# Recurrence of a hybrid encoder: which operand of the level products is stationary, and the order of the jobs beside them

## What is computed

```
def step(S, inp):
    r_t, w_t, k_t, v_t, a_t, b_t = inp
    sa = jnp.einsum('bhvk,bhk->bhv', S, a_t)
    S_new = S * w_t[:, :, None, :] + sa[..., None] * b_t[:, :, None, :] + v_t[..., None] * k_t[:, :, None, :]
    y = jnp.einsum('bhvk,bhk->bhv', S_new if inclusive else S, r_t)
    return S_new, y
```

## Time and profile before

| | us |
|---|---|
| median of 3 runs | 1944.28 (1942.8 to 1944.61) |
| the profiled execution | 1947.11 |
| its span | 1945.0 |
| the recurrence in it, from the first A to the last Y | 316.0 |
| one of its later chunks | 37.6 |

### The profile page before, as it was taken

One profiled execution on the slowest core, in us unless ns is written; L12 is line 12 of the kernel. 1 busy time (PEld: TensorE's weight loads), 2 busy tenths in 40 slices (PEclk: granted clock), 3 DMA queues, 4 the chain that ended last, 5 costly groups with the idle time before them and its releaser, 6 DMA issues.

```text
span 1945.0 us, 22750 instructions
## 1 busy us (share of the span) xinstructions
PE 1763.7 (91%) x8988; PEld 1261.4 (65%) x8988; DVE 827.2 (43%) x1193; ACT 555.5 (29%) x1058; POOL 320.7 (16%) x263
## 2 busy tenths in 40 slices
PE   2999978789999996888888997999999999999995
PEld 2888736544444433676676444888888888888884
DVE  7224348765534426545553646211211121133555
ACT  3111167734343322433432012111111111122331
POOL 1700011146000004455452015200000000000000
PEclk8999999989999997788887998999999999999998
DMA  4310000000000000000001300411111111144333
GB/s 187 130 54 32 11 29 1 12 5 4 8 4 4 0 0 14 2 2 2 2 2 53 153 11 11 152 43 43 52 56 43 43 51 57 56 149 138 95 95 115
DMA packets 24277, 93.49 MB, mean 48 GB/s; under 512 B 2752, under 2 KB 5120, under 8 KB 23568
## 3 DMA queue, kind: packets, MB, share of 16 engines
q1 hardware_dynamic: 23744, 87.27, 13.0%
q0 software_dynamic: 464, 5.28, 0.7%
HBM read 79.92 MB, written 12.58 MB: 48 GB/s over the span
## 4 chain that ended last, share of the span: by engine, by line
PE 84%; DVE 9%; ACT 4%; issue 2%; DMA 1%; POOL 0%; SPq 0%; DVEq 0%; ACTq 0%; POOLq 0%
PE psum L1842 25%; PE psum L1868 12%; PE psum L1456 9%; PE psum L1597 5%; PE psum L1793 5%; PE psum L1607 5%; PE psum L1474 2%; PE psum L1556 2%; PE psum L1538 1%; PE psum L1579 1%; PE psum L1693 1%; PE psum L1519 1%; PE psum L1481 1%; DVE stats L1138 1%; PE psum L1761 1%
## 5 line engine op out<-in xcount | busy, mean ns | idle before, releaser
L1842 PE MATMUL psum<-h_hi,w_hi 128*128 128x512 f32 x704 | 275.2, 391 | 11.7 <-DVE h_lo L1336 11.7
L1842 PE MATMUL psum<-h_lo,w_hi 128*128 128x512 f32 x704 | 274.4, 390 | 0.0
L1842 PE MATMUL psum<-h_hi,w_lo 128*128 128x512 f32 x704 | 274.4, 390 | 0.0
L1369 DVE TENSOR_TENSOR arena<-psum,arena 128x1024 f32 (+1 forms) x22 | 27.0, 1225 | 391.3 <-ACT arena L914 391.3
L1842 PEld LDWEIGHTS psum<-h_hi,w_hi 128*128 128x128 f32 x704 | 132.6, 188 | 39.7 <-DVE h_lo L1336 12.0
L1842 PEld LDWEIGHTS psum<-h_lo,w_hi 128*128 128x128 f32 x704 | 132.6, 188 | 27.8 <-issue 0.2
L1842 PEld LDWEIGHTS psum<-h_hi,w_lo 128*128 128x128 f32 x704 | 132.5, 188 | 27.5
L628 POOL TENSOR_TENSOR arena<-arena,consts 128x512 f32<-128x512 f32 x64 | 80.2, 1270 | 321.9 <-ACT arena L846 321.9
L1868 PE MATMUL psum<-wd_hi,act_lo 128*128 128x512 f32 x336 | 130.7, 389 | 0.0
L1868 PE MATMUL psum<-wd_lo,act_hi 128*128 128x512 f32 x336 | 130.7, 389 | 0.0
L1868 PE MATMUL psum<-wd_hi,act_hi 128*128 128x512 f32 x336 | 130.7, 389 | 0.0
(11 more groups left out here) (265 smaller groups left out, 2895.8 us busy)
## 6 DMA issues: line engine op xcount, KB each, us to landing
arena<-in_w_down SPq DMA_DIRECT2D x44, 512.0 KB, 3.6
arena<-in_w_gate SPq DMA_DIRECT2D x22, 512.0 KB, 3.5
arena<-in_w_up SPq DMA_DIRECT2D x22, 512.0 KB, 4.6
arena<-in_w_in SPq DMA_DIRECT2D x15, 512.0 KB, 3.6
arena<-in_x SPq DMA_DIRECT2D x8, 512.0 KB, 10.1
resid_spill<-arena POOLq DMA_DIRECT2D x1, 4096.0 KB, 12.9
arena<-in_w_out SPq DMA_DIRECT2D x8, 512.0 KB, 6.2
arena<-resid_spill SPq DMA_DIRECT2D x1, 4096.0 KB, 19.5
```

Source lines behind the costliest of these rows:

```text
L1842: mm = pe.matmul(bank(4 * b + 2 * n + hf), w[b][n][:, P * k:P * k + P], x[k][:, cols], start=(k == 0 and i == 0), stop=(k == KT - 1 and i ...
```

## The change

A level has two hops left for each direction, G and E. In both the full 128x128 matrix of a head is stationary (Lev in G, Xt in E) and the compact 32 columns move (Xc in G, Gc in E). The result comes out in the layout in which it is wanted, so GT and D's second transpose are gone, with their ACT copies. Xc and Xtc exist twice, by the parity of the chunk, so that A of the next chunk can be taken up earlier. G5 takes Xc and D5 Xtc directly. The blocks of the full X and Xt are put in place by 12 small POOL copies for each chunk (own_blocks). G6 of both directions is one job, with the two directions' products in turn on different tiles of the array; so is D6. AV and AZ become one job AX that accumulates in PSUM, without a DVE addition. The jobs beside the chain get new places (BESIDE), U of the chunk before right behind G of level 1.

```diff
-HOPS = [(kind, m) for m in range(1, 5) for kind in ("G", "GT", "D", "E")] + [(kind, 0) for kind in ("G5", "D5", "G6", "D6")]
-BACK = {0: ("AZ0", "AZ1"), 1: ("U0",), 2: ("U1",), 3: ("Y0",), 4: ("Y1",), 5: ("S0",), 6: ("S1",)}
-FRONT = {7: ("tok0",), 8: ("V0", "V1"), 9: ("tok1",), 10: ("KR0",), 11: ("KR1",), 12: ("AV0",), 13: ("AV1",), 14: ("R0",),
-         15: ("R1",)}
-AHEAD = {16: ("A0",), 17: ("A1",)}
+HOPS = [(kind, m) for m in range(1, 5) for kind in ("G", "E")] + [(kind, 0) for kind in ("G5", "D5", "G6", "D6")]
+BESIDE = {0: ("U0-",), 1: ("U1-", "Y0-", "A0+"), 2: ("KR0",), 3: ("Y1-",), 4: ("KR1",), 5: ("A1+", "S0-", "S1-"),
+          6: ("V1",), 7: ("V0", "tok0"), 8: ("R0", "tok1"), 9: ("AX1",), 10: ("AX0",), 11: ("R1",)}
+TOGETHER = ("G6", "D6")
...
-            jobs += [(kind, d, m, i) for d in range(2)]
-            if i:
-                jobs += named(BACK.get(n, ()), i - 1)
-            jobs += named(FRONT.get(n, ()), i)
-            if i + 1 < NT:
-                jobs += named(AHEAD.get(n, ()), i + 1)
-    return jobs + named(("AZ0", "AZ1", "U0", "U1", "Y0", "Y1"), NT - 1)
+            if i < NT:
+                jobs += [(kind, d, m, i) for d in range(1 if kind in TOGETHER else 2)]
+            for name in BESIDE.get(n, ()):
+                j = i + name.count("+") - name.count("-")
+                kind_d = name.strip("+-")
+                if 0 <= j < NT and not (kind_d[0] == "S" and j == NT - 1):
+                    jobs.append((kind_d[:-1], int(kind_d[-1]), 0, j))
...
+        elif kind in TOGETHER:
+            banks[job] = (4 + turn[0], 6 + turn[1])
+            turn = [1 - turn[0], 1 - turn[1]]
...
-        Xc, Xtc, Gc, G5 = ([heads4(32) for d in range(2)] for _ in range(4))
-        Gr, Dr = ([small(P) for d in range(2)] for _ in range(2))
+        Xcs, Xtcs = ([[heads4(32) for d in range(2)] for n in range(2)] for _ in range(2))
+        Gc, G5 = ([heads4(32) for d in range(2)] for _ in range(2))
...
+            def own_blocks(full, compact, which, i):
+
+                for d in range(2):
+                    pool.wait_ge(xt_ready, XTC_AT[d, 4, i])
+                    rows64 = halves_of(d)[which]
+                    for at in (rows64.start, rows64.start + 32):
+                        rows = slice(at, at + 32)
+                        pool.tensor_copy(full[d][rows, :, rows], compact[d][rows]).then_inc(xt_full, 1)
...
+                if i:
+                    pool.wait_ge(xt_full, OTHER_HALF_AT[i - 1])
...
+                pool.wait_ge(xt_full, XT_AT[1, 4, i])
+                own_blocks(X, Xcs[i % 2], 1, i)
+                own_blocks(Xt, Xtcs[i % 2], 0, i)
+                own_blocks(X, Xcs[i % 2], 0, i)
...
-                elif kind in ("G", "GT", "D"):
-                    dst = {"G": Gr[d], "GT": Gc[d].rearrange("p h c -> p (h c)"), "D": Dr[d]}[kind]
-                    ins = act.activation(dst, psum[:, b0, 0:P], ACT.Copy)
-                elif kind == "E" and m == 4:
-                    taken(act, job)
-                    for p in range(4):
-                        rows = slice(32 * p, 32 * p + 32)
-                        act.activation(X[d][rows, :, 32 * p:32 * p + 32], Xc[d][rows], ACT.Copy).then_inc(x_full, 1)
+                elif kind == "G":
+                    ins = act.activation(Gc[d].rearrange("p h c -> p (h c)"), psum[:, b0, 0:P], ACT.Copy)
...
+                    if i >= 2:
+                        v.wait_ge(xt_full, OTHER_HALF_AT[i - 2])
...
-                    if m == 4:
-                        v.wait_ge(xt_ready, XTC_AT[d, m, i])
-                        v.tensor_tensor(Xt[d].rearrange("p h (k c) -> p h k c", c=32), spread(Xtc[d]), own_block,
-                                        ALU.mult).then_inc(xt_ready, 1)
...
-                elif kind == "AZ":
-                    taken(v, ("AV", d, 0, i))
-                    v.tensor_tensor(Xs[d].rearrange("p h c -> p (h c)"), bank(b0, 256),
-                                    AVs[d].rearrange("p h c -> p (h c)"), ALU.add).then_inc(out_v, 1)
...
-                        mm = pe.matmul(psum[32 * h:32 * h + 32, b0, 0:P], Xc[d][:, h, :], Lev[d][m % 2][:, h, :],
-                                       start=True, stop=True, skip_group_check=True)
-                elif kind in ("GT", "E"):
-                    taken(pe, ("G" if kind == "GT" else "D", d, m, i))
-                    mm = pe.transpose(quarter, (Gr if kind == "GT" else Dr)[d], ident)
-                elif kind == "D":
-                    taken(pe, ("GT", d, m, i))
+                        mm = pe.matmul(psum[:, b0, 32 * h:32 * h + 32], Lev[d][m % 2][:, h, :], Xc[d][:, h, :],
+                                       start=True, stop=True)
+                elif kind == "E":
+                    taken(pe, ("G", d, m, i))
                     pe.wait_ge(xt_full, XT_AT[d, m, i])
                     for h in range(4):
-                        mm = pe.matmul(psum[32 * h:32 * h + 32, b0, 0:P], Gc[d][:, h, :], Xt[d][:, h, :],
-                                       start=True, stop=True, skip_group_check=True)
+                        mm = pe.matmul(psum[:, b0, 32 * h:32 * h + 32], Xt[d][:, h, :], Gc[d][:, h, :],
+                                       start=True, stop=True)
...
+                elif kind in TOGETHER:
+                    if kind == "G6":
+                        taken(pe, ("D5", 0, 0, i))
+                        taken(pe, ("D5", 1, 0, i))
+                        pe.wait_ge(xt_full, FIRST_HALF_AT[i])
+                    else:
+                        taken(pe, ("G6", 0, 0, i))
+                        pe.wait_ge(xt_full, TURNED_OWN_AT[i])
+                        pe.wait_ge(xt_ready, TURNED_AT[1, i])
+                    for h in range(4):
+                        for d in range(2):
+                            dst, src = halves_of(d)
+                            out = psum[dst, banks[d], 64 * h:64 * h + 64]
+                            if kind == "G6":
...
-                elif kind == "AV":
+                elif kind == "AX":
                     taken(pe, ("KR", d, 0, i))
                     taken(pe, ("V", d, 0, i))
                     for h in range(4):
-                        mm = pe.matmul(psum[:, b0, 64 * h:64 * h + 64], KAm[d][:, h, :],
-                                       tokv[d][:, h // 2, 64 * (h % 2):64 * (h % 2) + 64], start=True, stop=True)
-                elif kind == "AZ":
+                        pe.matmul(psum[:, b0, 64 * h:64 * h + 64], KAm[d][:, h, :],
+                                  tokv[d][:, h // 2, 64 * (h % 2):64 * (h % 2) + 64], start=(h == 0), stop=False,
+                                  skip_group_check=True)
                     if i:
                         taken(pe, ("S", d, 0, i - 1))
                     else:
                         pe.wait_ge(y_cleared, 5)
                     for hp in range(2):
                         mm = pe.matmul(psum[:, b0, P * hp:P * hp + P], At[:, 2 * d + hp, at_chunk(d, i)], Zs[d][:, hp, :],
-                                       start=True, stop=True)
+                                       start=False, stop=True, skip_group_check=True)
```

More of the change, by code:

```diff
@@ L89 @@
 LEV_AT = {(d, m, i): 8 * i + 2 * (m - 1) + d + 1 for i in range(NT) for m in range(1, 5) for d in range(2)}
[L90 to L93, removed]
+XT_AT = {(d, m, i): 20 * i + 2 * (m - 1) + d + 1 for i in range(NT) for m in range(1, 5) for d in range(2)}
+XTC_AT = {(d, m, i): 10 * i + 2 * (m - 1) + d + 1 for i in range(NT) for m in range(1, 5) for d in range(2)}
+TURNED_AT = {(d, i): 10 * i + d + 9 for i in range(NT) for d in range(2)}
+FIRST_HALF_AT = {i: 20 * i + 12 for i in range(NT)}
+TURNED_OWN_AT = {i: 20 * i + 16 for i in range(NT)}
+OTHER_HALF_AT = {i: 20 * i + 20 for i in range(NT)}
 def bank_plan():
@@ L311, in hybrid_encoder @@
         at[1] += at[0]
-        AVs, Us = ([pairs2() for d in range(2)] for _ in range(2))
+        Us = [pairs2() for d in range(2)]
         G6 = [heads4(64) for d in range(2)]
@@ L862, in _ @@
                 elif kind == "G6":
-                    dst, src = halves_of(d)
-                    ins = act.activation(G6[d][dst].rearrange("p h c -> p (h c)"), psum[dst, b0, 0:256], ACT.Copy)
+                    for d in range(2):
+                        dst, src = halves_of(d)
+                        ins = act.activation(G6[d][dst].rearrange("p h c -> p (h c)"), psum[dst, BANKS[job][d], 0:256], ACT.Copy)
                 elif kind == "tok":
                     ins = act.activation(tokm[d].rearrange("p q s c -> p (q s c)"), bank(b0), ACT.Copy)
-                elif kind in ("V", "AV", "U"):
-                    dst = {"V": tokv, "AV": AVs, "U": Us}[kind][d]
+                elif kind in ("V", "AX", "U"):
+                    dst = {"V": tokv, "AX": Xs, "U": Us}[kind][d]
                     ins = act.activation(dst.rearrange("p h c -> p (h c)"), bank(b0, 256), ACT.Copy)
@@ L1260, in _ @@
                 elif kind == "D6":
-                    dst, src = halves_of(d)
```

(34 more changed lines are left out.)

28 lines of the change are left out of this document (13 added, 15 removed).

## The result

| | before | after |
|---|---|---|
| median of the runs, us | 1944.05 (1942.8 to 1944.61, 4 runs) | 2053.25 (2052.66 to 2072.74, 4 runs) |
| span of the profiled execution, us | 1945.0 | 2051.5 |
| the recurrence in it, us | 316.0 | 421.8 |

The change makes the kernel slower by 5.9%: the ratio is 1.0587, 95% interval 1.0525 to 1.0649. The span grew by 106.5 us and the recurrence alone by 105.8 us, so hardly anything else moved. One of the four executions took 2072.74 us, at a mean granted clock of 0.895 against 0.901 to 0.904 in the others.

The account below looks back on a forecast made before the run. PE's jobs, the waits between them and the half clock were taken to bound the kernel. The recurrence: 8.4 + 50.6 + 431.2 - 2.5 + 10.4 = 498.1 us against 316.0, 182 us more: 2126 us, range 1965 to 2150.

Parts of the forecast that it names:

- the load bounds the product: G and E: the 128-column weight load sets the time, so 32 moving columns don't shorten it; 114 ns an instruction.
- PE's work at both clocks: PE's jobs in a later chunk, summed: 33.9 us at full clock, 64.6 us at half.
- The waits: PE's waits within a chunk, 5.1 us before, were taken to vanish behind PE's own jobs.
- The sign that G6 of both directions would take less time than one had alone: G6 as one job on different tiles: both directions in less time than one alone before.
- Without the clock the change is worth 3.7 us a chunk: Later chunk of the recurrence: 37.6 us before less 33.9 us of PE work at full clock.
- The forecast's own case: Recurrence mostly at half clock, granted clock near 0.55, 498 us; kernel 2126 us; chance 0.58 together with half clock throughout.
- So a chunk takes 61.6 us: Later chunk: 64.6 us at half clock less 3 us for the clock returning around A, S0 and S1.
- E4: E of level 4, in the thin stretch where the returned clock was to be lost again; its return worth 3 us a chunk.
- rival 1: Clock returns at S, is lost at G of level 1: 50.9 us a chunk, 2053 us; chance 0.20.
- rival 2: Clock falls once a chunk for 10.2 us, as before: 39.0 us a chunk, 1967 us; chance 0.06.
- four half-clock cases: Recurrence mostly at half clock 2126 us, back from S to level 1 2053, one fall a chunk 1967, half throughout 2147.
- Rival 3: PE without waits gets full clock in the recurrence, keeping 3.7 us a chunk: 1917 us; chance 0.14.

Follow-up runs that it names:

- wide: Changed kernel with all 128 compact columns moving in G and E, only 32 of each head's result columns read: 1920.5 us.
- wide_g: Changed kernel with 128 columns moving in G only, E keeping 32: 1927.8 us.
- half: Changed kernel with 64 columns (two heads) moving in G and E, of which 32 are used: 1955.7 us.
- wide_serial: As wide, but G6 and D6 issued direction after direction inside their one job, not in turn: 1923.2 us.
- shift1: Changed kernel with one DVE memset added between the first A and the first level, to start the levels some 2 us later: 2061.9 us.
- shift2: Changed kernel with two DVE memsets added between the first A and the first level, to start the levels some 4 us later: 1988.2 us.

## Why the prediction was right, and where it wasn't

**The range and the direction** held: slower, 2053.25 us inside 1965 to 2150. The mechanism behind them, that the load bounds the product and that few streamed columns cost the clock, was right and is shown by wide, wide_g and half. What exactly the chip counts stays open: the columns that move past the array and the results that it writes grew together in these runs.

**PE's work at both clocks** was right. A level job was put at 0.91 and 1.70 us and took 0.86 and 1.71 (half of the 16 instructions of G, and 8 times 213 ns). A chunk at full clock was put at 33.9 us and took 34.8 in wide, 34.5 in half. At half clock it was put at 64.6; chunk 3 took 60.5 us with a clock of 0.53, which is 64 us for 0.50. Chunk 0 with what precedes it was put at 59.0 us and took 58.4.

**The waits** were taken at nothing, and PE had none from the first G to the last Y. POOL's 12 copies for a chunk took 289 ns each, against 286. Three terms of the sum at full clock were mis-sized, and cancel in the main: G6 and D6 took 0.61 us each against 0.45, the two AX 3.06 us against 2.7, G5 and D5 1.64 us against 2.2. The sign that G6 of both directions would take less time than one had alone didn't appear, as in wide_serial one direction alone takes half of 0.89 us.

**"Without the clock the change is worth 3.7 us a chunk"** sets a changed chunk at full clock, 33.9 us, against the 37.6 us of before, which hold 5.1 us of half clock's cost by the prediction's own count. Against 32.5 us, an estimate for a chunk of before at full clock throughout, the changed chunk is 1.4 us longer. By this estimate what wide gains on the kernel before comes from the clock as well.

**The forecast's own case was wrong.** The step that failed is "So a chunk takes 61.6 us", which a clock near 0.55 and 498 us for the recurrence follow from; measured were 0.63 and 421.8 us. I let the clock come back at S and be lost with G4, V1 and E4, worth 3 us. It did come back there, at 844.4 and 1015.1, but was then kept for 17 us, through E4, G5 and D5 to E of level 1. That is rival 1, chunks of 52.8 and 53.1 us against its 50.9. Others lost it at once: chunk 3 with 60.5 us is the forecast's case. And chunks 5 and 6 with 37.6 us, clock lost for 6.8 us only, are rival 2, which I had put at 39.0. So three of my four half-clock cases occurred side by side in one execution. The forecast, 182 us more, was 1.7 times the 109 measured.

**Rival 1's 2053 us is the measured time, by luck.** It assumed seven equal chunks of 50.9 us; the seven took 37.6 to 60.5, and only their mean is the same. shift1 and shift2 ran from 1984 to 2083 us with the same work. What I should have seen is that the case isn't fixed by the order of the jobs alone: the seven chunks have the same order. That the moment at which the clock changes against the jobs decides is my reading, and not shown by itself. A single number for this kernel was worth less than its range.

**Rival 3**, full clock throughout, was put at 1917 us for the changed kernel and didn't occur there. wide is that case made real, 1920.5 us. The rule of the Trainium skill that the prediction names beside it (TensorE: Matmul & The Clock Gate, The HAM clock gate), that a busy PE is released to full clock, doesn't hold in the row of 804.7 to 844.4: busy for 39.70 of 39.70 us, clock 0.50.

**What the prediction missed**: that the cure was in its own argument. If the load bounds the product, more moving columns, up to 128, are nearly free, and the clock they hold is worth 133 us.

## What to carry to other kernels

Where a weight load bounds a float32 product, moving more columns cost next to nothing here (107 ns an instruction with 32, 112 with 128; more than 128 wasn't tried there), and streaming too few cost the clock of the jobs around it as well; ask of a denser schedule how much it streams, not only whether the engine waits. A transposed product that saves hops can still lose if it gives up column strips that worked at once: here the old level products with the rest of the change are the fastest version. And when a chunk of equal work takes 37.6 us once and 60.5 us another time, repeat the run, and shift the work by a few microseconds, before believing a single measured number.

## What the runs showed of the hardware

- The clock can stay at 0.50 while PE is busy without a gap: 39.7 us in chunk 1 of the changed kernel. At the start of half it stayed there for 98.2 us with 91.87 us busy.
- The same stream of jobs can hold the full clock and fail to regain it: half, 98.2 us at 0.50, then 225.6 us at 1.00, with S of chunk 1 at the rise.
- A float32 instruction with 128 stationary columns takes 107 ns at full clock with 32 moving columns, 108 with 64 and 112 with 128. At half clock, 16 of them in a row took 3.55 us with 32 (with the first one's start), 3.60 with 64 and 3.71 with 128.
- The number of moving columns in the level products set the time of the otherwise same kernel: 2053, 1956, 1928 and 1920 us for 32, 64, 32 and 128, 128 columns.
- 64x64 tiles of the two directions, issued in turn, take 0.61 us for 16 instructions, one direction after the other 0.89 us: an overlap of a third, not a half.
